# The second half of the gated block's value projection as seven block products, with spatial-weight preparation and the last statistics moved into the projection behind it

## The chip, the cores and the metric

The kernel runs on one core of one Trainium2 chip. The metric is the device time of one execution in microseconds (us), as a median of several runs. All times below come from those runs or from one execution taken by the profiler.

## The reference, cut to what matters

The program is a four-layer network on 512 tokens of width 1024: latent attention, stick-breaking attention, a gated block with a spatial mixing of tokens, and windowed attention. The change lies in the gated block alone:

```python
def gmlp_mixer(h, w_in, ln_g, ln_b, ws, bs, w_out):      # h: 512 x 1024, w_in: 1024 x 6144
    z = h @ w_in
    u, v, g = jnp.split(z, 3, axis=-1)                    # each 512 x 2048
    v = layer_norm(v, ln_g, ln_b)
    v = v.reshape(b, nc, CHUNK, A_GROUPS, A_GROUP_DIM)    # 4 chunks of 128 tokens, 16 groups of 128
    wsm = jnp.where(causal[None], ws, jnp.zeros_like(ws))
    sv = jnp.einsum('gts,bcsgd->bctgd', wsm, v) + bs.T[:, :, None]
    y = u * sv.reshape(b, s, A_WIDTH) * jax.nn.silu(g)
    return y @ w_out
```

Here h is the RMS-normed residual stream. All inputs are 32-bit floats.

## The kernel before, in words

**Matmuls in three parts.** TensorE multiplies values that are each split into a high and a low part (w_hi and w_lo for weights, a0h and a0l for activations). One product of 128x128 by 512 columns is three matmuls: high by high, high by low, low by high (`three`, L572 to L576). ScalarE (ACT) makes the high part of each weight slab with a copy (L1233), VectorE (DVE) the low part with a subtraction (L1857). Both hold two slabs of 128x1024: slot r % 2 for load r.

**Projections.** A `Linear` (L372 to L399) has groups of 512 output columns, and a group has loads of two k tiles each, four loads for K = 1024. A group fills four PSUM banks; groups alternate between banks 0 to 3 and 4 to 7. For each k tile TensorE (PE) computes four tiles, so that a group is 8 x 4 x 3 = 96 matmuls and a load 24. PE waits for `lo_ready` at each load, and at the start of group G for the readers of group G - 2, which had the same banks (L604 to L606). ACT may overwrite a slot when PE has finished the load two before (L1232: `ring_used` at least r - 1).

**Order by hand.** Every engine's program is written out in order. In the helper `linear` of ACT (L1252) and DVE (L1878), step j of group g first splits load g * 4 + j + 1, so the load after the one of this step; then, at j = 0 and 1 of every group but the first, it reads two banks each of the group before; then it takes one item of the list `extra`:

```python
split_to(L.load0 + g * L.lpg + j + 1, i)
if g and j < 2:
    reads(g - 1, range(4) if L.lpg == 1 else range(2 * j, 2 * j + 2), i)
if extra:
    extra.pop(0)()
```

With `between=True` DVE reads the last group's banks 0 and 1 with a split behind each; ACT has no such option.

**The gated block.** `g_v` (L390) is the value projection: four groups, token-major, so banks hold 128 tokens by 512 columns. ACT evicts each bank with the token's norm factor (`v_read`, L1696), DVE takes bn_stats of it (`v_stats`, L2390). `g_u` (L391) follows, with four groups that DVE reads with the norm row (`normed_to`, L1969), then the spatial product (L1057 to L1067) and `g_g`.

Beside g_v lies the preparation of the spatial weights: ACT makes high parts (`ws_hi`, L1721), DVE low parts (`ws_low`, L2396), PE multiplies them by minus one's matrix for their column sums (`ws_sums`, L1040 to L1050, eight matmuls, called ahead of k tile 6 of the second group of g_v), and DVE multiplies the four banks of sums by a gain and adjusts a bias (`ws_bias`, L2399 to L2409). The four banks of sums are those that the third group of g_v uses, so PE waits at its start: `if G == lin["g_v"].group0 + 2: pe.wait_ge(S("ws_bias"), 4)` (L599). On DVE `ws_bias` is the eighth item of `extra`, so it comes at the last step of the second group. `v_moments` and `v_shift` (first two items in g_u) join the statistics, POOL takes the root (L2796), and ACT normalizes v_g in four instructions (`v_normed`, L1713, items three to six of g_u).

**A projection by seven products is already there.** `sh_v` (L383, 1024 columns of another layer) goes by `fast` (L896), a Strassen-like scheme of Winograd's form: the operands are cut into 2x2 blocks, four sums of activation blocks and four of weight blocks are made, and seven block products of 4 k tiles x 2 tiles x 3 = 24 matmuls each replace eight. Its loads are half slabs (28 loads of 128x512, six matmuls each). The activation sums are made beside the projection ahead, `sh_k`: ACT scales activations (`gained`, L1574), DVE adds (`sums`, L2264), both split (`sums_hi` L1566, `sums_lo` L2253). The weight sums are made by transfers that add: SyncE (SP) loads four slabs after the norm of sh_k (`load_sums`, L534 to L539, issued between loads 5 and 6 of sh_k), POOL issues four adding transfers onto them (`weight_sums`, L2731 to L2739), and DVE adds twice two more (`weight_sum`, L2276). ACT evicts the first products (L1582), DVE adds the others onto them (L2285); both are called `fast_tokens` (L1578, L2278).

In sh_k only DVE reads banks; in g_v ACT reads them first and DVE works on what ACT wrote.

Of the kernel before, what the change touches and what calls it, by code (L numbers as in the profile page):

```python
# [8 lines left out]
ALU = mybir.AluOpType  # L9
# [75 lines left out]
class Fast:  # L85
# [5 lines left out]
    def __init__(self, extra, sums):  # L91
        self.extra, self.sums = extra, sums
        self.home, self.landed = {}, {}

# [38 lines left out]
def build(nc, ctx, ins, out, cols):  # L133
# [53 lines left out]
    def put(name, shape, kb, dt=F32, of=None):  # L187
# [42 lines left out]
        + [put("sv_slot3", [P, 2, T], 80)]  # L230
    kT_sh = put("kT_sh", [P, KD, T], 32)
# [134 lines left out]
    def columns(a, b, step=T):  # L366
# [16 lines left out]
        Linear("sh_v", w_sh, 8, columns(D, 2 * D), True, A0, items("h_kv"), fast=Fast(sv_slots, (s_hi, s_lo))),  # L383
# [6 lines left out]
        Linear("g_v", w_g, 8, columns(GW, 2 * GW), True, A0, items("h_g")),  # L390
# [13 lines left out]
               "sh_v": ("sums_out", 4),  # L404
               "gate1": ("g_read", 0), "g_v": ("g_read", 8), "g_u": ("g_read", 24), "g_g": ("g_read", 40)}
# [4 lines left out]
    for L in LINEARS:  # L410
# [97 lines left out]
    def _(sp_):  # L508
# [36 lines left out]
        for L in LINEARS[1:]:  # L545
# [25 lines left out]
    def _(pe):  # L571
# [13 lines left out]
        def group(L, g, i=None, before={}):  # L585
# [13 lines left out]
            if G == lin["g_v"].group0 + 2:  # L599
                pe.wait_ge(S("ws_bias"), 4)  # L600
# [295 lines left out]
        def fast(L):  # L896
# [155 lines left out]
        linear("g_v", 2, second={6: ws_sums})  # L1052
        linear("g_u")
# [143 lines left out]
    def _(act):  # L1197
# [10 lines left out]
        def split(r, i=None):  # L1208
# [353 lines left out]
        def sums_hi(qs):  # L1562
            def do():
                for q in qs:
                    act.wait_ge(S("s_ok"), q + 1)
                    act.activation(s_hi[:, q, :, :], s_f[:, q, :, :], ACT.Copy).then_inc(S("s_hi"), 1)  # L1566
            return do

        def gained(sets, name):
            def do():  # L1570
                for q in sets:
                    k0, t0 = ((4, T // 2), (0, T // 2), (0, 0), (4, 0))[q]
                    for k in range(4):
                        last = act.activation(s_f[:, q, k, :], xT[:, k0 + k, t0:t0 + T // 2], ACT.Identity, scale=gain(name, k0 + k))  # L1574
# [3 lines left out]
        def fast_tokens(L, t):  # L1578


            def evict(to, bank, m, sem):
                act.activation(to, bank, ACT.Identity, scale=nrm[:, m:m + 1]).then_inc(S(sem), 1)  # L1582

            a = ps[4 * (L.group0 % 2):4 * (L.group0 % 2) + 2]
            for j in range(Fast.N):
                split_to(L.load0 + j)
                if j == 7:
                    act.wait_ge(S("ring_used"), L.load0 + 4)
                    act.wait_ge(S("nrm_ok"), 2)
                    for m in range(2):  # L1590
                        evict(t[:, m, T:D], a[m][:, :], m, "first_out")
                    for m in range(2):
                        evict(t[:, 2 + m, 0:T], a[m][:, :], 2 + m, "first_out")
                if j == 23:
                    act.wait_ge(S("ring_used"), L.load0 + 20)
                    for m in range(2):
                        evict(t[:, m, 0:T], a[m][:, :], m, "first_out")

        linear("sh_k", None, [nothing, nothing, gained((0, 1), "h_kv"), gained((2, 3), "h_kv"), hi_two("h_sb", 0), hi_two("h_sb", 1),
                               lambda: (sums_hi((0, 1))(), hi_two("h_sb", 2)()), lambda: (sums_hi((2, 3))(), hi_two("h_sb", 3)())])  # L1600
        fast_tokens(lin["sh_v"], v_sh)
# [122 lines left out]
        linear("g_v", v_read, [nothing, nothing] + [ws_hi(q) for q in range(4)] + [nothing] * 10)  # L1724
        linear("g_u", extra=[nothing, nothing] + [v_normed(m) for m in range(MB)], near=True)
# [105 lines left out]
    def _(dve):  # L1831
# [417 lines left out]
        def sums_lo(qs):  # L2249
            def do():  # L2250
                for q in qs:
                    dve.wait_ge(S("s_hi"), 4 + q + 1)
                    dve.tensor_tensor(s_lo[:, q, :, :], s_f[:, q, :, :], s_hi[:, q, :, :], ALU.subtract).then_inc(S("s_lo"), 1)  # L2253
            return do

        def sums(qs):
# [10 lines left out]
        def weight_sum(name, p):

            b, count, read = {"t2": ("b22", None, 6), "t4": ("b21", 5, 10)}[name]
            at = lin["sh_v"].fast  # L2270
            to = at.home["t", p]
            if count:
                dve.wait_ge(S("s_ok"), count + p)
            dve.wait_ge(*at.landed[b, p])
            dve.wait_ge(S("lo_ready"), lin["sh_v"].load0 + read + 2 * p)
            dve.tensor_tensor(to[:, :, :], to[:, :, :], at.home[b, p][:, :, :], ALU.add).then_inc(S("s_ok"), 1)  # L2276

        def fast_tokens(L, t):  # L2278
# [5 lines left out]
            def add(to, bank, m, other, sem, op=ALU.add):  # L2284
                dve.scalar_tensor_tensor(to, bank[:, :], nrm[:, m:m + 1], other, ALU.mult, op).then_inc(S(sem), 1)  # L2285

            one, two = slice(0, T), slice(T, D)
            done = "sums_out"
            for j in range(Fast.N):
# [5 lines left out]
                if j == 15:  # L2295
                    dve.wait_ge(S("ring_used"), L.load0 + 12)
                    dve.wait_ge(S("first_out"), 4)
                    for m in range(2):
                        add(t[:, 2 + m, one], b[m], 2 + m, t[:, 2 + m, one], done)
                if j == 16:  # L2300
                    for m in range(2):
                        add(t[:, m, two], b[m], m, t[:, m, two], done)
                if j == 18:
                    dve.wait_ge(S("ring_used"), L.load0 + 16)
                    dve.wait_ge(S(done), 2)
                    for m in range(2):
                        add(t[:, 2 + m, two], d[m], 2 + m, t[:, 2 + m, one], done)
                if j == 19:
                    dve.wait_ge(S(done), 6)
                    for m in range(2):  # L2310
                        add(t[:, 2 + m, two], c[m], 2 + m, t[:, 2 + m, two], done, ALU.subtract)
                if j == 27:
                    dve.wait_ge(S("ring_used"), L.load0 + 24)
                    for m in range(2):
                        add(t[:, m, two], c[m], m, t[:, m, two], done, ALU.subtract)
            split_to(L.load0 + Fast.N)
            dve.wait_ge(S("ring_used"), L.load0 + Fast.N)
            for m in range(2):
                add(t[:, 2 + m, one], d[m], 2 + m, t[:, 2 + m, one], done)

        linear("sh_k", normed_to(kT_sh, 1),
               [nothing, nothing, norm(1, 1e-6, "sh_k"), sums((0,)), lambda: (sums((1, 2, 3))(), lo_two("h_sb", 0)()), lo_two("h_sb", 1),
                lambda: (sums_lo((0, 1))(), lo_two("h_sb", 2)()), lambda: (sums_lo((2, 3))(), lo_two("h_sb", 3)())], between=True)
        fast_tokens(lin["sh_v"], v_sh)
# [66 lines left out]

        def ws_low(q):
# [18 lines left out]
        linear("g_v", v_stats, [nothing, nothing, norm(2, 1e-5, "g_v")] + [ws_low(q) for q in range(4)] + [ws_bias])  # L2411
# [32 lines left out]
        linear("g_u", normed_to(ug, 2), [v_moments, v_shift], near=True)  # L2444
# [171 lines left out]
    def _(pool):  # L2616
# [178 lines left out]
        root(nrm, MB, "nrm_in", 3, "nrm_ok")  # L2795
        root(bn_rs, MB, "bn_in", 1, "bn_ok")  # L2796
# [126 lines left out]
```

## Time and profile before

| | us |
|---|---|
| median of 3 runs | 1309.9 (1309.74 to 1310.02) |
| the profiled execution, its own time | 1309.88 |
| span of that execution, first to last instruction | 1308.1 |
| PE busy | 1290.3 (99% of the span) |
| DVE busy | 787.4 (60%) |
| ACT busy | 660.3 (50%) |
| POOL busy | 349.2 (27%) |

The time is 1.8 us longer than the span. In the timeline rows each line has a start in us from the span's start, a duration in us, the engine, the source line, the operation, what it writes and reads, and how many instructions were merged; a bracket gives the idle time ahead of it and what ended it. Matmuls are pipelined, so one's duration reaches into the next: the distance between starts tells their pace. The rows themselves stand behind the diff.

### The profile page before, as it was taken

What the parts mean: (1) busy time and instruction counts of PE and PEld (TensorE: products, weight loads), DVE (VectorE), ACT (ScalarE), POOL (GpSimd) and SP (SyncE); (2) the same over time, 40 slices, a digit from 0 to 9 for tenths busy, and PEclk for the clock granted to TensorE, in tenths of its full rate; (3) what the DMA queues carried; (4) which work ended last, traced back from release to release, by engine and by line L of the source; (5) the groups of instructions that cost most, each with busy time, mean ns of one, the idle gap of its engine ahead of it and who ended that gap; (6) DMA issues with size and microseconds to landing.
All of it is one profiled execution on the core that took longest, in us unless ns stands there. A gap on an engine that the chain in (4) does not pass through costs nothing.

```text
span 1308.1 us, 17925 instructions
## 1 busy us (share of the span) xinstructions
PE 1290.3 (99%) x6454; PEld 1081.5 (83%) x6454; DVE 787.4 (60%) x1253; ACT 660.3 (50%) x1202; POOL 349.2 (27%) x397
## 2 busy tenths in 40 slices
PE   7999999999999999999999999999999999999998
PEld 6997778788888888887888888889888888888886
DVE  5646888735698235897444653335457236578843
ACT  5379888624664326997244523414244234355632
POOL 2238877400010008773000000000000000668620
PEclk9999999999999999999999999999999999999999
DMA  5332100132192232001323323331332321421111
GB/s 195 85 106 65 45 25 14 49 104 96 58 257 80 98 97 81 1 0 33 113 97 97 97 86 99 97 96 59 99 98 95 123 97 49 130 65 49 33 65 65
DMA packets 72500, 107.81 MB, mean 82 GB/s; under 512 B 3572, under 2 KB 31464, under 8 KB 72296
## 3 DMA queue, kind: packets, MB, share of 16 engines
q1 hardware_dynamic: 70128, 100.49, 24.4%
q0 software_dynamic: 2176, 6.27, 1.9%
q8 instruction: 47, 0.77, 0.3%
q14 instruction: 29, 0.24, 0.1%
q10 hardware_dynamic: 120, 0.05, 0.0%
HBM read 104.70 MB, written 2.10 MB: 82 GB/s over the span
## 4 chain that ended last, share of the span: by engine, by line
PE 91%; DVE 4%; issue 2%; ACT 1%; DMA 1%; SPq 0%; DVEq 0%; POOL 0%; ACTq 0%; POOLq 0%
PE ps L574 24%; PE ps L576 24%; PE ps L575 24%; PE ps L777 3%; PE ps L1121 2%; PE ps L973 2%; PE ps L790 1%; PE ps L963 1%; PE ps L1065 1%; PE ps L756 1%; PE ps L964 1%; PE ps L804 1%; DVE sp L2334 1%; PE ps L805 1%; DMA x_tok<-in_x 1%
## 5 line engine op out<-in xcount | busy, mean ns | idle before, releaser
L1857 DVE TENSOR_TENSOR w_lo<-stage,w_hi 128x1024 fp32r<-128x1024 f32 (+4 forms) x180 | 214.3, 1191 | 374.7 <-ACT w_hi L1233 374.5
L1233 ACT ACTIVATE w_hi<-stage 128x1024 fp32r<-128x1024 f32 (+4 forms) x180 | 182.7, 1015 | 417.8 <-PE ps L576 412.5
L574 PE MATMUL ps<-a0h,w_hi 128*128 128x512 f32 x512 | 204.6, 400 | 0.8 <-DVE q_lo L2521 0.8
L576 PE MATMUL ps<-a0h,w_lo 128*128 128x512 f32 x512 | 199.9, 390 | 0.0
L575 PE MATMUL ps<-a0l,w_hi 128*128 128x512 f32 x512 | 199.5, 390 | 0.0
L2623 POOL TENSOR_TENSOR small<-small 128x16 f32<-128x16 f32 (+2 forms) x14 | 32.3, 2313 | 387.9 <-DVE small L1941 284.4
L576 PEld LDWEIGHTS ps<-a0h,w_lo 128*128 128x128 f32 x512 | 96.1, 188 | 20.6
L574 PEld LDWEIGHTS ps<-a0h,w_hi 128*128 128x128 f32 x512 | 96.2, 188 | 20.1 <-issue 1.3
L575 PEld LDWEIGHTS ps<-a0l,w_hi 128*128 128x128 f32 x512 | 96.3, 188 | 18.3 <-issue 0.2
L574 PE MATMUL ps<-w_hi,a0h 128*128 128x512 f32 (+1 forms) x280 | 106.3, 380 | 0.1
L576 PE MATMUL ps<-w_hi,a0l 128*128 128x512 f32 (+1 forms) x280 | 104.3, 373 | 0.0
L575 PE MATMUL ps<-w_lo,a0h 128*128 128x512 f32 (+1 forms) x280 | 104.2, 372 | 0.0
L574 PE MATMUL ps<-a1h,w_hi 128*128 128x512 f32 x256 | 100.0, 391 | 0.3 <-DVE w_lo L1857 0.3
L576 PE MATMUL ps<-a1h,w_lo 128*128 128x512 f32 x256 | 99.6, 389 | 0.0
L575 PE MATMUL ps<-a1l,w_hi 128*128 128x512 f32 x256 | 99.6, 389 | 0.0
L574 PEld LDWEIGHTS ps<-w_hi,a0h 128*128 128x128 f32 x280 | 52.6, 188 | 10.1 <-issue 0.9
L575 PEld LDWEIGHTS ps<-w_lo,a0h 128*128 128x128 f32 x280 | 52.6, 188 | 9.1 <-issue 0.7
L576 PEld LDWEIGHTS ps<-w_hi,a0l 128*128 128x128 f32 x280 | 52.5, 188 | 8.5
L574 PEld LDWEIGHTS ps<-a1h,w_hi 128*128 128x128 f32 x256 | 48.0, 188 | 11.0 <-DVE w_lo L1857 0.8
L576 PEld LDWEIGHTS ps<-a1h,w_lo 128*128 128x128 f32 x256 | 48.0, 188 | 10.1
L575 PEld LDWEIGHTS ps<-a1l,w_hi 128*128 128x128 f32 x256 | 48.1, 188 | 9.8
L574 PE MATMUL ps<-yh,w_hi 128*128 128x512 f32 x128 | 49.9, 390 | 0.0
(347 smaller groups left out, 2969.5 us busy)
## 6 DMA issues: line engine op xcount, KB each, us to landing
stage<-in_a_w_in SPq DMA_DIRECT2D x48, 512.0 KB, 3.7
stage<-in_ple_w_gate SPq DMA_DIRECT2D x16, 512.0 KB, 3.3
stage<-in_sb_w_in SPq DMA_DIRECT2D x16, 512.0 KB, 3.7
stage<-in_a_w_out SPq DMA_DIRECT2D x16, 512.0 KB, 3.3
stage<-in_b_w_in SPq DMA_DIRECT2D x16, 512.0 KB, 3.7
stage<-in_w_kv_shared SPq DMA_DIRECT2D x14, 512.0 KB, 4.3
stage<-in_mla_w_in SPq DMA_DIRECT2D x8, 512.0 KB, 3.9
stage<-in_sb_w_out SPq DMA_DIRECT2D x8, 512.0 KB, 3.3
```

The source lines that it names most:

```text
L574: pe.matmul(bank, wh, mh, start=start and not seeded, stop=False, skip_group_check=seeded)
L575: pe.matmul(bank, wh, ml, start=False, stop=False, skip_group_check=seeded)
L576: return pe.matmul(bank, wl, mh, start=False, stop=stop, skip_group_check=seeded)
L756: t = pe.transpose(ps[bank][0:QK, m * P:(m + 1) * P], ring[s][:, m, :], ident)
L777: pe.matmul(ps[b][:, c:c + n], qT[s][0:QK, j * P:(j + 1) * P], kT[s][0:QK, 0:n], start=j != 0, stop=False, skip_group_check=True)
L790: t = pe.transpose(ps[3 + b][:, c + (q - j) * P:c + (q - j + 1) * P], pr[:, QRY_COL[q] + j * P:QRY_COL[q] + (j + 1) * P], ident)
L804: pe.matmul(ps[6][:, j * P:T], v_hl[h % 2][:, j, :], prT_h[:, at], start=j == 0, stop=False, skip_group_check=True)
L973: t = pe.matmul(ps[6 + s][:, j * P:T], v_pair2[:, j, :], a_T[s][:, KEY_COL[j]:KEY_COL[j] + T - j * P], start=j == 0, stop=j == MB - 1, ski ...
L1121: t = pe.matmul(ps[W_OUT][:, j * P:j * P + n], v_dup[:, e, j, :], pwT[s][:, j, 0:n], start=j == 0, stop=j == MB - 1, skip_group_check=True)
L1233: act.activation(slab(w_hi[r % 2], L, nk, w), slab(stage[q], L, nk, w), ACT.Copy).then_inc(S("hi_ready"), 1)
L1857: dve.tensor_tensor(slab(w_lo[r % 2], L, nk, w), slab(stage[stage_of[r][0]], L, nk, w), slab(w_hi[r % 2], L, nk, w), ALU.subtract)\
L2623: return pool.tensor_tensor(ap, ap, minus_half[:, 0:n], ALU.pow).then_inc(S(ready), 1)
```

## The change

g_v keeps its first two groups. Its other two become a projection of their own, `g_w`, which goes by `fast` (seven products) with outputs in v_g. The helpers of sh_v are given the projection, its semaphore offsets, its buffers and its output slices as parameters, and g_w gets the same activation sums and weight sums beside g_v. ws_hi, ws_low, ws_sums and ws_bias move from g_v into g_u, and the bn_stats of g_w's halves come in g_u as `fast_stats`. The diff, cut to its core:

```diff
+    g_f = put("g_f", [P, 4, 4, T // 2], 48)
+    g_lo = put("g_lo", [P, 4, 4, T // 2], 48, F32R)
...
-        Linear("g_v", w_g, 8, columns(GW, 2 * GW), True, A0, items("h_g")),
+        Linear("g_v", w_g, 8, columns(GW, GW + D), True, A0, items("h_g")),
+        Linear("g_w", w_g, 8, columns(GW + D, 2 * GW), True, A0, items("h_g"),
+               fast=Fast(1, 3, sv_slots, g_f, (s_hi, g_lo), lambda m, half: v_g[:, 8 + 4 * half:12 + 4 * half, m, :],
+                         lambda bank: bank[:, :].rearrange("p (g d) -> p g d", g=4))),
...
-               "sh_v": ("sums_out", 4),
-               "gate1": ("g_read", 0), "g_v": ("g_read", 8), "g_u": ("g_read", 24), "g_g": ("g_read", 40)}
+               "sh_v": ("sums_out", 4), "g_w": ("sums_out", 16),
+               "gate1": ("g_read", 0), "g_v": ("g_read", 8), "g_u": ("g_read", 16), "g_g": ("g_read", 32)}
...
@@ SyncE
-            sp_.wait_ge(S("rstd_done"), 2)
+            sp_.wait_ge(S("rstd_done"), L.fast.norm)
...
-                    if r == lin["sh_k"].load0 + 5:
-                        load_sums(lin["sh_v"])
+                    for ahead, L2 in (("sh_k", "sh_v"), ("g_v", "g_w")):
+                        if r == lin[ahead].load0 + 5:
+                            load_sums(lin[L2])
...
@@ TensorE
-            if G == lin["g_v"].group0 + 2:
+            if G == lin["g_u"].group0 + 1:
                 pe.wait_ge(S("ws_bias"), 4)
...
         def ws_sums():
 
-            G = lin["g_v"].group0
+            G = lin["g_u"].group0 + 1
             pe.wait_ge(S("ws_ok"), 4)
-            pe.wait_ge(S(group_read[G][0]), group_read[G][1])
+            pe.wait_ge(S(group_read[G - 2][0]), group_read[G - 2][1])
...
-        linear("g_v", 2, second={6: ws_sums})
-        linear("g_u")
+        linear("g_v", 2)
+        fast(lin["g_w"])
+        linear("g_u", before={6: ws_sums})
...
@@ ScalarE
-        linear("g_v", v_read, [nothing, nothing] + [ws_hi(q) for q in range(4)] + [nothing] * 10)
-        linear("g_u", extra=[nothing, nothing] + [v_normed(m) for m in range(MB)], near=True)
+        gw = lin["g_w"]
+        linear("g_v", v_read, [nothing, nothing, gained(gw, (0, 1), "h_g"), gained(gw, (2, 3), "h_g"), nothing, nothing,
+                               sums_hi(gw, (0, 1)), sums_hi(gw, (2, 3))])
+        fast_tokens(gw)
+        linear("g_u", extra=[lambda: [ws_hi(q)() for q in range(4)], nothing, nothing, nothing] + [v_normed(m) for m in range(MB)], near=True)
...
@@ VectorE
+        def fast_stats():
+
+            dve.wait_ge(S("sums_out"), gw.fast.count("sums_out", 12))
+            dve.wait_ge(S("first_out"), gw.fast.count("first_out", 6))
+            for n in range(MB):
+                for g in (2, 3):
+                    dve.bn_stats(bn_st[:, n, g, :], v_g[:, 4 * g:4 * g + 4, n, :]).then_inc(S("bn_done"), 1)
+
...
         def ws_bias():
 
-            G = lin["g_v"].group0
+            G = lin["g_u"].group0 + 1
...
-        linear("g_v", v_stats, [nothing, nothing, norm(2, 1e-5, "g_v")] + [ws_low(q) for q in range(4)] + [ws_bias])
+        gw = lin["g_w"]
+        linear("g_v", v_stats, [nothing, nothing, norm(2, 1e-5, "g_v"), sums(gw, (0,)), sums(gw, (1, 2, 3)), nothing,
+                                sums_lo(gw, (0, 1)), sums_lo(gw, (2, 3))], between=True)
+        fast_tokens(gw)
...
-        linear("g_u", normed_to(ug, 2), [v_moments, v_shift], near=True)
+        linear("g_u", normed_to(ug, 2), [fast_stats, lambda: [ws_low(q)() for q in range(4)], v_moments, v_shift, ws_bias], near=True)
...
@@ GpSimd
         root(nrm, MB, "nrm_in", 3, "nrm_ok")
+        weight_sums(lin["g_w"])
         root(bn_rs, MB, "bn_in", 1, "bn_ok")
```

## Rows read from the trace of the kernel before

**Rows 1.** the page: busy time, and engines of the chain that ended last
```profile
PE 1290.3 (99%) x6454; PEld 1081.5 (83%) x6454; DVE 787.4 (60%) x1253; ACT 660.3 (50%) x1202; POOL 349.2 (27%) x397
...
PE 91%; DVE 4%; issue 2%; ACT 1%; DMA 1%; SPq 0%; DVEq 0%; POOL 0%; ACTq 0%; POOLq 0%
```

**Rows 2.** busy time by windows: span, engines, PEclk, DMA share, GB/s
```profile
790.00:812.00 22.00, 22.00 (x98) 18.20 (x97) 7.30 (x8) 6.56 (x8) 0.00 (x0) 1.00 0.35 100
```

**Rows 3.** timeline of PE: first matmul of g_v's third group, of g_u's first two
```profile
769.18 0.39 PE L574 MATMUL ps<-w_hi,a0h 128*128 128x512 f32 x1
...
812.70 0.39 PE L574 MATMUL ps<-a0h,w_hi 128*128 128x512 f32 x1
...
834.46 0.39 PE L574 MATMUL ps<-a0h,w_hi 128*128 128x512 f32 x1
```

**Rows 4.** timeline of PE: sh_v's first matmul, the first behind sh_v (sb_gate's)
```profile
384.23 0.39 PE L574 MATMUL ps<-w_hi,a0h 128*128 128x512 f32 x1
...
422.55 0.47 PE L574 MATMUL ps<-a1h,w_hi 128*128 128x512 f32 x1
```

**Rows 5.** timeline of SP, POOL, ACT in sh_k: weight sums, the load behind
```profile
359.90 1.91 SPq L539 DMA_DIRECT2D sv_slot<-in_w_kv_shared  x4
...
368.93 5.01 POOL L2739 DMA_DIRECT2D sv_slot<-in_w_kv_shared  x4 [11.39 <-DMA sv_slot<-in_w_kv_shared]
...
370.01 1.07 ACT L1233 ACTIVATE w_hi<-stage 128x1024 fp32r<-128x1024 f32 x1 [5.00 <-DMA stage<-in_w_kv_shared]
...
388.20 2.36 ACT L1227 ACTIVATE w_hi<-sv_slot 128x512 fp32r<-128x512 f32 x4 [2.56 <-DMA sv_slot<-in_w_kv_shared]
```

**Rows 6.** timeline of ACT and DVE in sh_v: half slabs, high and low
```profile
384.49 1.16 ACT L1227 ACTIVATE w_hi<-stage 128x512 fp32r<-128x512 f32 x2 [1.15 <-PE ps L576]
...
385.48 0.68 DVE L1855 TENSOR_TENSOR w_lo<-stage,w_hi 128x512 fp32r<-128x512 f32 x1
```

**Rows 7.** timeline of ACT at g_v's end, DVE in the group behind
```profile
812.96 1.06 ACT L1233 ACTIVATE w_hi<-stage 128x1024 fp32r<-128x1024 f32 x1 [4.38 <-PE ps L576]
...
813.92 2.40 ACT L1696 ACTIVATE v_g<-ps,small 128x512 f32<-128x512 f32 x4
...
815.19 2.46 DVE L2390 BATCH_NORM_STATS2 small<-v_g 128x6 f32<-128x512 f32 x4
```

**Rows 8.** timeline of DVE behind sh_v's end
```profile
423.96 1.22 DVE L1857 TENSOR_TENSOR w_lo<-stage,w_hi 128x1024 fp32r<-128x1024 f32 x1
```

**Rows 9.** timeline of DVE at g_v's second group's end: ws_bias
```profile
764.34 2.48 DVE L2406 TENSOR_TENSOR ws_b<-ps,gains 128x512 f32<-128x512 f32 x4
```

**Rows 10.** timeline of ACT and DVE at the start of g_u's second group
```profile
834.72 1.06 ACT L1233 ACTIVATE w_hi<-stage 128x1024 fp32r<-128x1024 f32 x1 [2.38 <-PE ps L576]
...
835.81 1.23 DVE L1857 TENSOR_TENSOR w_lo<-stage,w_hi 128x1024 fp32r<-128x1024 f32 x1 [4.21 <-ACT w_hi L1233]
...
836.95 1.28 DVE L1969 TENSOR_TENSOR ug<-ps,rstd 128x512 f32<-128x512 f32 x2
```

**Rows 11.** timeline of PE: a wait for DVE, and the matmul behind it
```profile
508.31 0.50 PE L574 MATMUL ps<-a1h,w_hi 128*128 128x512 f32 x1 [0.33 <-DVE w_lo L1857]
...
508.65 0.40 PE L575 MATMUL ps<-a1l,w_hi 128*128 128x512 f32 x1
```

**Rows 12.** PE's last matmul; then windows (columns as in rows 2) behind it
```profile
1301.75 0.39 PE L576 MATMUL ps<-w_hi,o_bl 128*128 128x512 f32 x1
...
1305.50:1306.00 0.50, 0.00 (x0) 0.00 (x0) 0.00 (x0) 0.00 (x0) 0.00 (x0) 0.66 1.05 389
...
1306.00:1307.00 1.00, 0.00 (x0) 0.00 (x0) 0.00 (x0) 0.00 (x0) 0.00 (x0) 0.50 1.00 385
```

**Rows 13.** timeline of PE: the first products of the span
```profile
8.32 0.80 PE L574 MATMUL ps<-pTh,w_hi 128*128 128x512 f32 x1 [1.16 <-DVE w_lo L1851]
...
8.91 0.63 PE L575 MATMUL ps<-pTl,w_hi 128*128 128x512 f32 x1
...
12.18 0.40 PE L574 MATMUL ps<-pTh,w_hi 128*128 128x512 f32 x1
```

More of the change, by code:

```diff
@@ L89, with __init__, count @@
     N = 4 * len(SPLITS)
-    def __init__(self, extra, sums):
-        self.extra, self.sums = extra, sums
+    def __init__(self, nth, norm, extra, total, sums, out, shape):
+        self.nth, self.norm, self.extra, self.total, self.sums, self.out, self.shape = nth, norm, extra, total, sums, out, shape
         self.home, self.landed = {}, {}
+    def count(self, name, n):
+        return n + self.nth * {"sums_in": 64, "adds_in": 64, "s_hi": 8, "s_ok": 8, "s_lo": 4, "first_out": 6, "sums_out": 12}[name]
     def source(self, j):
@@ L382, in build @@
         Linear("sh_k", w_sh, 8, columns(0, D), False, A0, items("h_kv")),
-        Linear("sh_v", w_sh, 8, columns(D, 2 * D), True, A0, items("h_kv"), fast=Fast(sv_slots, (s_hi, s_lo))),
+        Linear("sh_v", w_sh, 8, columns(D, 2 * D), True, A0, items("h_kv"),
+               fast=Fast(0, 2, sv_slots, s_f, (s_hi, s_lo), lambda m, half: v_sh[:, m, half * T:half * T + T], lambda bank: bank[:, :])),
         Linear("sb_gate", w_sb, 8, columns(D, 2 * D), False, A1, items("h_sb")),
@@ L437, in build @@
                     if name in ("t", "b12"):
-                        to, landed, need = L.fast.extra[p + 2 * (name == "t")], (S("adds_in"), 64), None
+                        to, landed, need = L.fast.extra[p + 2 * (name == "t")], (S("adds_in"), L.fast.count("adds_in", 64)), None
                     else:
@@ L1560, in hi_two, with sums_hi, gained @@
             return do
-        def sums_hi(qs):
+        def sums_hi(L, qs):
             def do():
                 for q in qs:
-                    act.wait_ge(S("s_ok"), q + 1)
-                    act.activation(s_hi[:, q, :, :], s_f[:, q, :, :], ACT.Copy).then_inc(S("s_hi"), 1)
+                    act.wait_ge(S("s_ok"), L.fast.count("s_ok", q + 1))
+                    act.activation(L.fast.sums[0][:, q, :, :], L.fast.total[:, q, :, :], ACT.Copy).then_inc(S("s_hi"), 1)
             return do
-        def gained(sets, name):
+        def gained(L, sets, name):
             def do():
@@ L1573, in do, with fast_tokens, evict @@
                     for k in range(4):
-                        last = act.activation(s_f[:, q, k, :], xT[:, k0 + k, t0:t0 + T // 2], ACT.Identity, scale=gain(name, k0 + k))
+                        last = act.activation(L.fast.total[:, q, k, :], xT[:, k0 + k, t0:t0 + T // 2], ACT.Identity, scale=gain(name, k0 + k))
                     last.then_inc(S("s_hi"), 1)
             return do
-        def fast_tokens(L, t):
-            def evict(to, bank, m, sem):
-                act.activation(to, bank, ACT.Identity, scale=nrm[:, m:m + 1]).then_inc(S(sem), 1)
+        def fast_tokens(L):
+            out = L.fast.out
+            def evict(to, bank, m):
+                act.activation(to, L.fast.shape(bank), ACT.Identity, scale=nrm[:, m:m + 1]).then_inc(S("first_out"), 1)
             a = ps[4 * (L.group0 % 2):4 * (L.group0 % 2) + 2]
@@ L1588, in fast_tokens @@
                     act.wait_ge(S("ring_used"), L.load0 + 4)
-                    act.wait_ge(S("nrm_ok"), 2)
+                    act.wait_ge(S("nrm_ok"), L.fast.norm)
                     for m in range(2):
-                        evict(t[:, m, T:D], a[m][:, :], m, "first_out")
+                        evict(out(m, 1), a[m], m)
                     for m in range(2):
-                        evict(t[:, 2 + m, 0:T], a[m][:, :], 2 + m, "first_out")
+                        evict(out(2 + m, 0), a[m], 2 + m)
                 if j == 23:
@@ L1596, in fast_tokens @@
                     for m in range(2):
[L1597 to L1601, printed above, removed]
+                        evict(out(m, 0), a[m], m)
+        sv = lin["sh_v"]
+        linear("sh_k", None, [nothing, nothing, gained(sv, (0, 1), "h_kv"), gained(sv, (2, 3), "h_kv"), hi_two("h_sb", 0), hi_two("h_sb", 1),
+                               lambda: (sums_hi(sv, (0, 1))(), hi_two("h_sb", 2)()), lambda: (sums_hi(sv, (2, 3))(), hi_two("h_sb", 3)())])
+        fast_tokens(sv)
         linear("sb_gate", silu_gate)
@@ L2248, in _, with sums_lo @@
         rest_of_layer(0, 1, "h_kv")
[L2249 removed]
+        def sums_lo(L, qs):
             def do():
                 for q in qs:
[L2252 to L2256 removed]
+                    dve.wait_ge(S("s_hi"), L.fast.count("s_hi", 4 + q + 1))
+                    dve.tensor_tensor(L.fast.sums[1][:, q, :, :], L.fast.total[:, q, :, :], L.fast.sums[0][:, q, :, :], ALU.subtract)\
+                       .then_inc(S("s_lo"), 1)
+            return do
@@ L2265, in sums @@
             return do
[L2267 to L2276, printed above, removed]
@@ L2278, in fast_tokens, with weight_sum, add @@
-        def fast_tokens(L, t):
+        def fast_tokens(L):
             here, there = ps[4 * (L.group0 % 2):4 * (L.group0 % 2) + 4], ps[4 * (1 - L.group0 % 2):4 * (1 - L.group0 % 2) + 4]
             b, c, d = here[2:4], there[0:2], there[2:4]
[L2284 to L2288, printed above, removed]
+            out, count = L.fast.out, L.fast.count
+            def weight_sum(name, p):
+                other, after, read = {"t2": ("b22", None, 6), "t4": ("b21", 5, 10)}[name]
+                to = L.fast.home["t", p]
+                if after:
+                    dve.wait_ge(S("s_ok"), count("s_ok", after + p))
+                dve.wait_ge(*L.fast.landed[other, p])
+                dve.wait_ge(S("lo_ready"), L.load0 + read + 2 * p)
+                dve.tensor_tensor(to[:, :, :], to[:, :, :], L.fast.home[other, p][:, :, :], ALU.add).then_inc(S("s_ok"), 1)
+            def add(to, bank, m, other, op=ALU.add):
+                dve.scalar_tensor_tensor(to, L.fast.shape(bank), nrm[:, m:m + 1], other, ALU.mult, op).then_inc(S("sums_out"), 1)
@@ L2314, in fast_tokens @@
                     for m in range(2):
-                        add(t[:, m, two], c[m], m, t[:, m, two], done, ALU.subtract)
+                        add(out(m, 1), c[m], m, out(m, 1), ALU.subtract)
             split_to(L.load0 + Fast.N)
@@ L2318, in fast_tokens @@
             for m in range(2):
-                add(t[:, 2 + m, one], d[m], 2 + m, t[:, 2 + m, one], done)
+                add(out(2 + m, 0), d[m], 2 + m, out(2 + m, 0))
+        sv = lin["sh_v"]
         linear("sh_k", normed_to(kT_sh, 1),
-               [nothing, nothing, norm(1, 1e-6, "sh_k"), sums((0,)), lambda: (sums((1, 2, 3))(), lo_two("h_sb", 0)()), lo_two("h_sb", 1),
-                lambda: (sums_lo((0, 1))(), lo_two("h_sb", 2)()), lambda: (sums_lo((2, 3))(), lo_two("h_sb", 3)())], between=True)
-        fast_tokens(lin["sh_v"], v_sh)
+               [nothing, nothing, norm(1, 1e-6, "sh_k"), sums(sv, (0,)), lambda: (sums(sv, (1, 2, 3))(), lo_two("h_sb", 0)()), lo_two("h_sb", 1),
+                lambda: (sums_lo(sv, (0, 1))(), lo_two("h_sb", 2)()), lambda: (sums_lo(sv, (2, 3))(), lo_two("h_sb", 3)())], between=True)
+        fast_tokens(sv)
         linear("sb_gate", normed_to(sg, 1))
```

38 lines of the change are left out of this document (20 added, 18 removed).

## The prediction

> **What bounds the kernel now.** I read the page first: TensorE (PE) is busy for 99% of the span and holds 91% of the chain that ended last [rows 1]. So time goes down only where PE issues less, and any new wait of PE adds to it. Next I asked for windows inside g_v: PE is busy for the whole stretch at a granted clock of 1.00, DVE and ACT for a third of it [rows 2]. Then the timeline of PE for the pace. A matmul is listed with 0.39 us, but matmuls overlap, and that is not what one costs. From the first matmul of g_v's third group to the first of g_u are 192 matmuls in 812.70 - 769.18 = 43.52 us, 0.2267 us each, with no gap [rows 3]. A group of 96 takes 21.76 us, a full load of 24 takes 5.44, a half slab of six 1.36.
>
> **What the change takes away.** Two groups are 192 matmuls; seven products of 24 are 168. That is 24 x 0.2267 = **5.44 us less**. (By the listed 0.39 it would be 9.4, which is wrong for the reason above.) Can seven products run at PE's pace? In sh_v they do: 422.55 - 384.23 = 38.32 us for 168 matmuls, against 38.08 at the pace above [rows 4]. What surrounds g_w differs from that at two places, its start and the group after it.
>
> **What is moved or added without price.** Activation sums (gained, sums, sums_hi, sums_lo) lie beside g_v at the same steps as beside sh_k, which fed sh_v in time and had the splits for another layer to do as well. SP waits at L539 for the norm ahead of four transfers, with g_v's last two loads and all half slabs queued behind. In sh_k those transfers started at 359.90 and the load behind them came at 370.01 [rows 5]; split in 1.07 and 1.2 us it was ready at about 372.3, and PE wanted it at 384.23 - 10.88 = 373.35. That cover is 1 us; beyond it every us late is one lost. POOL issues the four adding transfers in 5.01 us [rows 5] and has nothing behind them until the statistics' root in g_u. They had landed when ACT went on at 388.20, 3.97 us into sh_v [rows 5]. fast_stats stands on DVE ahead of g_u's third slab: behind sh_v DVE was done with the second slab 2.63 us after PE went on (423.96 + 1.22 - 422.55) [rows 4, 8]; eight bn_stats of 0.62 (2.46 for four [rows 7]) bring that to 7.55, the third slab to 8.8, and PE wants it at 10.88. ws_low (four like a half slab's 0.68 [rows 6]) ends by 11.5, ws_hi on ACT before that; ws_sums is ahead of k tile 6, at 16.3, its eight matmuls are as many as before. v_normed is two steps later, with two groups of g_u still to run.
>
> **A wait at the start of g_w.** ACT now evicts g_v's last group (in sh_k it had nothing to read) before it makes the high part of g_w's third half slab, whose slot is free only when PE is through with g_v. ACT comes 0.26 us after PE's first matmul of what follows (812.96 against 812.70); four evictions are 2.40 [rows 3, 7]; the high part 0.58, the low part 0.68 [rows 6]; 0.05 to PE: 3.97. PE is through two half slabs at 2.72, so it waits 1.25. Then DVE owes, by its order, a bn_stats, a low part, two bn_stats and the low part for the fifth half slab: 3.92 + 0.62 + 0.68 + 1.23 + 0.68 + 0.05 = 7.2, where PE comes at 3.97 + 2.72 + 0.1 = 6.8, the 0.1 being what a restart costs (0.34 instead of 0.23 to the next start [rows 11]). With the overlaps I take **1.6 us** for both; ends 0.2 (as sh_v) and 2.5 (no overlap, and 0.5 from a later landing).
>
> **A wait in front of g_u's second group.** ws_sums fills the four banks of g_u's second group, so PE now waits there for ws_bias. On DVE ws_bias is the fifth item of g_u's list. Four items go with the four steps of the first group; the fifth comes at step 0 of the second, behind the split of that group's second load and behind two reads of the first group's banks. Both need the first group finished: the split's slot is free only then, and the reads ask for it. So PE stops at the end of the first group, and the whole of this chain lies bare, where before ws_bias ended about 2 us ahead of PE (764.34 + 2.48 against 769.18 [rows 3, 9]). Its price stands in the trace at the very place: PE would go on at 834.46 [rows 3]; ACT's high part starts at 834.72, DVE's low part at 835.81, the two reads at 836.95 and take 1.28 [rows 10]; four multiplications take 2.48 [rows 9]. That ends at 840.71, 6.25 late; with 0.05 to PE and 0.1 for the restart **6.4 us**. Ends 6.0 and 6.8. The fifth operation of ws_bias is not waited for.
>
> **The clock.** PE is then idle for 6.2 us. Before, it has no such pause within the work, so the price is bounded from its two ends. Behind its last matmul (ended 1302.14) the granted clock fell from 1.00 to 0.50 inside 1305.5 to 1306.0, about 3.5 us later [rows 12]; a pause of 6.2 us reaches past that. How the pace comes back shows at the span's start: eight starts from 8.91 to 12.18 took 3.27 us where 1.81 is usual, and the first 0.59 instead of 0.34 [rows 11, 13], so at about half the pace, in all 1.7 us lost. Ends: 0 (no fall) and twice that, 3.4; I take **1.7**, the one recovery that rows show. The Trainium skill (TensorE: Matmul & The Clock Gate, Part 1: The HAM clock gate (the "warmup" mystery)) states as a rule that an idle TensorE drops to half its clock and that only sustained activity releases it. By that rule the sum is the one with this term, without it the one of the first rival; the fall in rows 12 agrees, and no run here shows it for a pause between matmuls.
>
> **The sum.** -5.44 + 1.6 + 6.4 + 1.7 = +4.3 us. The profiled execution took 1309.88 (1.8 more than its span), so **1314.1**; the median of the runs, 1309.9, is the same to 0.02. The chain is PE's to the end, so nothing behind g_u gives back or adds.
>
> **Rivals.** (1) Both waits, but the clock stays up or costs nothing: +2.6, 1312.4. For it: the pause is not far longer than what the clock outlived in rows 12. Against: it is longer by almost 3 us. (2) On the other side: ws_bias comes before PE does. It has four operations, and their input is complete 5.4 us before the first group ends; if DVE reached them at step 3, as it did before in g_v, they would end in time, and only the first wait would be left: -5.44 + 1.6, **1306.0**. The point that decides is whether the fifth item runs ahead of the end of the first group; by the helper's order it can't, so this needs that I misread the list. (3) The adding transfers land late. w_g has rows three times as long as w_sh, and g_w has 1.9 us of slack (its fifth half slab is wanted at 7.2 - 1.3 = 5.9, they landed at 3.97); if they took 4 us more, PE would lose 2: 1316.2. Against: each row piece is as long as in sh_v. (4) The seven products do not shorten g_w, with all else as forecast: this would be 5 us worse, and rows 4 speak against it; I give it next to nothing.
>
> **How the numbers follow.** Forecast 0.70, rival 1 0.13, rival 2 0.09, rival 3 with all later stalls 0.08. The forecast's own range is 1312.9 to 1316.0 (first wait 1.2 to 2.0, second 6.0 to 6.8, clock 1.0 to 3.0). The range of 8 in 10 takes in rival 1 and a little of rival 3: 1312.0 to 1316.6; rival 2 stays out. What a measurement of this kernel tells from no change is about 0.2%, 2.6 us. Faster is rival 2 and little else: 0.09. Within 0.2% (up to 1312.5) are half of rival 1 and the low corner of the forecast: 0.12. Slower: 0.79.
>
> **What would show it.** In the changed kernel's timeline PE should pause about 1.2 us at g_w's third half slab with DVE's low part (L1855) as releaser, and about 6 us between g_u's first two groups with DVE's ws_bias as releaser, followed by about eight matmuls at starts 0.41 apart under a granted clock of 0.50. From g_w's first matmul to g_u's first there should be about 39.7 us. The forecast is wrong if the second pause is under 3 us, if the pace behind it is 0.23 at once, or if ACT waits for a transfer into sv_slot long after PE has run dry.

## The result and the profile after

The changed kernel takes 1315.01 us (median of six runs, 1314.44 to 1315.85), the kernel before 1309.97. The ratio is 1.0038 (95% interval 1.0027 to 1.005): slower, by 5.0 us. The profiled execution took 1314.71 us, its span is 1312.9, 4.8 more than before.

The page of the changed kernel, its busy times and the engines of the chain that ended last (before: [rows 1]):

```profile
PE 1287.7 (98%) x6430; PEld 1078.0 (82%) x6430; DVE 817.0 (62%) x1297; ACT 677.3 (52%) x1240; POOL 354.3 (27%) x401
...
PE 91%; DVE 5%; issue 2%; ACT 1%; DMA 1%; SPq 0%; DVEq 0%; POOL 0%; ACTq 0%; POOLq 0%
```

PE has 24 instructions fewer and is busy for 2.6 us less, yet the span is longer: the loss is in waits and in a slow stretch behind one of them. PE's waits, longest first (total, times, longest):

```profile
PE ps L585 <- DVE ws_b L2433: 6.1, 1, 6.1
...
PE ps L585 <- DVE w_lo L1873: 1.0, 1, 1.0
```

Before, neither stood in this view. The timeline of PE shows where they lie (a start in us, a duration in us; a bracket gives the idle time and its releaser). It runs from g_w's first matmul over its third and fifth half slab to g_u's first matmul, the last one of g_u's first group, the restart behind it, and the first of the spatial product:

```profile
767.48 0.39 PE L585 MATMUL ps<-w_hi,a0h 128*128 128x512 f32 x1
...
769.98 0.39 PE L587 MATMUL ps<-w_hi,a0l 128*128 128x512 f32 x1
771.41 0.50 PE L585 MATMUL ps<-w_hi,a0h 128*128 128x512 f32 x1 [1.04 <-DVE w_lo L1873]
...
774.03 0.39 PE L587 MATMUL ps<-w_hi,a0l 128*128 128x512 f32 x1
774.48 0.47 PE L585 MATMUL ps<-w_hi,s_hi 128*128 128x512 f32 x1
...
807.34 0.47 PE L585 MATMUL ps<-a0h,w_hi 128*128 128x512 f32 x1
...
830.89 0.39 PE L587 MATMUL ps<-a0h,w_lo 128*128 128x512 f32 x1
...
837.33 0.80 PE L585 MATMUL ps<-a0h,w_hi 128*128 128x512 f32 x1 [6.05 <-DVE ws_b L2433]
837.92 0.63 PE L586 MATMUL ps<-a0l,w_hi 128*128 128x512 f32 x1
...
840.91 0.58 PE L587 MATMUL ps<-a0h,w_lo 128*128 128x512 f32 x1
841.33 0.39 PE L585 MATMUL ps<-a0h,w_hi 128*128 128x512 f32 x1
...
904.60 1.61 PE L1078 MATMUL ps<-wsT,v_ring 128*128 x13
```

And of the kernel before, the first matmul of g_v's second group (to its third, at 769.18 [rows 3], are 96 matmuls and the eight of ws_sums) and the first of the spatial product:

```profile
745.52 0.39 PE L574 MATMUL ps<-w_hi,a0h 128*128 128x512 f32 x1
...
899.74 1.50 PE L1065 MATMUL ps<-wsT,v_ring 128*128 x12
```

Between g_w's first matmul and g_u's are 39.86 us, where 168 matmuls at 0.2267 are 38.08: 1.78 lost. From g_u's first matmul to its second group's are 29.99 us, where 96 matmuls and the eight of ws_sums (1.9, 769.18 less 745.52 and 21.76 before) are 23.66: 6.33 lost. From there to the spatial product are 67.27 us, before 899.74 - 834.46 = 65.28: 1.99 lost. With -5.44 for the products and 0.20 by which this execution was late already at g_v's start (721.80 against 721.60), that is -5.44 + 1.78 + 6.33 + 1.99 + 0.20 = 4.86 us, the whole of the difference at the spatial product (904.60 - 899.74).

The timelines of ACT and DVE around the first wait, at g_w's start:

```profile
767.68 2.42 ACT L1711 ACTIVATE v_g<-ps,small 128x512 f32<-128x512 f32 x4 [2.33 <-PE ps L587]
769.98 1.16 ACT L1240 ACTIVATE w_hi<-stage 128x512 fp32r<-128x512 f32 x2
771.09 1.15 ACT L1240 ACTIVATE w_hi<-sv_slot 128x512 fp32r<-128x512 f32 x2
```

```profile
770.66 0.69 DVE L1873 TENSOR_TENSOR w_lo<-stage,w_hi 128x512 fp32r<-128x512 f32 x1 [1.49 <-ACT w_hi L1240]
...
772.46 1.28 DVE L2409 BATCH_NORM_STATS2 small<-v_g 128x6 f32<-128x512 f32 x2
773.66 1.28 DVE L1873 TENSOR_TENSOR w_lo<-sv_slot,w_hi 128x512 fp32r<-128x512 f32 x2
```

Four evictions, then the high part, then the low part at 770.66, which PE got at 771.41. The added slabs had landed by 771.09, since ACT did not wait for them.

DVE ahead of the second wait, at the start of g_u's second group:

```profile
826.28 0.15 DVE L2457 SCALAR_TENSOR_TENSOR small<-small 128x4 f32<-128x4 f32 x1
832.46 1.23 DVE L1875 TENSOR_TENSOR w_lo<-stage,w_hi 128x1024 fp32r<-128x1024 f32 x1 [6.03 <-ACT w_hi L1246]
833.61 1.28 DVE L1987 TENSOR_TENSOR ug<-ps,rstd 128x512 f32<-128x512 f32 x2
834.81 2.47 DVE L2433 TENSOR_TENSOR ws_b<-ps,gains 128x512 f32<-128x512 f32 x4
```

DVE was idle for 6.03 us while PE worked off the first group; then the low part, the two reads and ws_bias ran one after another in front of an idle PE, with the durations of [rows 9, 10]. And the windows of that stretch (columns as in rows 2, PEclk is third from the right):

```profile
831.00:834.00 3.00, 0.28 (x2) 0.00 (x0) 1.54 (x2) 2.62 (x2) 0.00 (x0) 1.00 0.00 0
834.00:835.00 1.00, 0.00 (x0) 0.00 (x0) 1.00 (x3) 0.42 (x1) 0.00 (x0) 0.75 0.44 31
835.00:836.00 1.00, 0.00 (x0) 0.00 (x0) 1.00 (x2) 0.00 (x0) 0.00 (x0) 0.50 0.66 217
...
840.00:841.00 1.00, 1.00 (x4) 0.75 (x3) 0.00 (x0) 0.00 (x0) 0.00 (x0) 0.50 0.00 0
841.00:842.00 1.00, 1.00 (x5) 0.81 (x4) 0.00 (x0) 0.00 (x0) 0.00 (x0) 0.84 0.06 16
```

PE's last matmul ended at 831.28, the granted clock fell in the window 834 to 835, and PE restarted at half of it (1.2 GHz), with starts 0.43 apart until 841.33.

### The profile page after: what moved, and what is told of

The parts are those of the page before. It is cut to its first block, busy times and chain, and to the rows that moved or that the text cites. A ratio compares the mean times of both kernels' runs of the same rounds, so it can differ in the third digit from the quotient of the medians.

```text
span 1312.9 us, 17989 instructions
## 1 busy us (share of the span) xinstructions
PE 1287.7 (98%) x6430; PEld 1078.0 (82%) x6430; DVE 817.0 (62%) x1297; ACT 677.3 (52%) x1240; POOL 354.3 (27%) x401
## 4 chain that ended last, share of the span: by engine, by line
PE 91%; DVE 5%; issue 2%; ACT 1%; DMA 1%; SPq 0%; DVEq 0%; POOL 0%; ACTq 0%; POOLq 0%
PE ps L585 24%; PE ps L587 24%; PE ps L586 24%; PE ps L788 3%; PE ps L1134 2%; PE ps L985 2%; PE ps L801 1%; PE ps L975 1%; PE ps L976 1%; PE ps L1078 1%; PE ps L767 1%; PE ps L815 1%; DVE sp L2353 1%; PE ps L816 1%; DVE sp_l L2358 1%
## 5 line engine op out<-in xcount | busy, mean ns | idle before, releaser
L1875 DVE TENSOR_TENSOR w_lo<-stage,w_hi 128x1024 fp32r<-128x1024 f32 (+4 forms) x172 | 204.5, 1189 | 339.8 <-ACT w_hi L1246 339.5
L1246 ACT ACTIVATE w_hi<-stage 128x1024 fp32r<-128x1024 f32 (+4 forms) x172 | 174.0, 1011 | 387.2 <-PE ps L587 376.1
L585 PE MATMUL ps<-w_hi,a0h 128*128 128x512 f32 (+1 forms) x240 | 90.9, 379 | 1.2 <-DVE w_lo L1873 1.0
L587 PE MATMUL ps<-w_hi,a0l 128*128 128x512 f32 (+1 forms) x240 | 88.8, 370 | 0.0
L586 PE MATMUL ps<-w_lo,a0h 128*128 128x512 f32 (+1 forms) x240 | 88.7, 370 | 0.0
L585 PEld LDWEIGHTS ps<-w_hi,a0h 128*128 128x128 f32 x240 | 45.1, 188 | 10.0 <-DVE w_lo L1873 1.5
L586 PEld LDWEIGHTS ps<-w_lo,a0h 128*128 128x128 f32 x240 | 45.1, 188 | 7.4 <-issue 0.7
L587 PEld LDWEIGHTS ps<-w_hi,a0l 128*128 128x128 f32 x240 | 45.1, 188 | 7.0
```

Of the source, the lines that this page charges most:

```text
L585: pe.matmul(bank, wh, mh, start=start and not seeded, stop=False, skip_group_check=seeded)
L586: pe.matmul(bank, wh, ml, start=False, stop=False, skip_group_check=seeded)
L587: return pe.matmul(bank, wl, mh, start=False, stop=stop, skip_group_check=seeded)
L1246: act.activation(slab(w_hi[r % 2], L, nk, w), slab(stage[q], L, nk, w), ACT.Copy).then_inc(S("hi_ready"), 1)
L1875: dve.tensor_tensor(slab(w_lo[r % 2], L, nk, w), slab(stage[stage_of[r][0]], L, nk, w), slab(w_hi[r % 2], L, nk, w), ALU.subtract)\
```

## The experiments

Each is timed beside the kernel before on the same chip (1309.8 to 1310.0 us there). The theory: the two waits come from the order of the work, the second with a fall of the clock behind it. The rivals: DVE has too much to do in g_u's first group, wherever ws_bias stands; and a pause costs PE something at its restart that has nothing to do with the clock.

**ws_bias one step earlier (e1_bias_earlier).**

```diff
-[fast_stats, lambda: [ws_low(q)() for q in range(4)], v_moments, v_shift, ws_bias]
+[fast_stats, lambda: [ws_low(q)() for q in range(4)], v_moments, lambda: (v_shift(), ws_bias())]
```

> The changed kernel with ws_bias one step earlier on DVE (with v_shift, at the last step of g_u's first group). Order theory: PE's wait ahead of g_u's second group is there only because ws_bias stood behind work that needs the first group finished. Then it goes, and the slow clock behind it too: 1310.0 - 5.4 + 1.8 = about 1306.3 us. Load theory (DVE has too much to do in g_u's first group, bn_stats and ws_low, and is late wherever ws_bias stands): PE still waits 3 us or more, 1309 us or above.

1306.39 us, ratio 0.9972 (0.9961 to 0.9984). DVE's timeline there:

```profile
825.18 1.23 DVE L1875 TENSOR_TENSOR w_lo<-stage,w_hi 128x1024 fp32r<-128x1024 f32 x1 [3.47 <-ACT w_hi L1246]
826.32 0.15 DVE L2457 SCALAR_TENSOR_TENSOR small<-small 128x4 f32<-128x4 f32 x1
826.40 2.48 DVE L2433 TENSOR_TENSOR ws_b<-ps,gains 128x512 f32<-128x512 f32 x4
```

ws_bias is done at 828.88. PE has no gap at the seam, where its starts are 0.23 apart:

```profile
831.16 0.39 PE L585 MATMUL ps<-a0h,w_hi 128*128 128x512 f32 x1
831.39 0.39 PE L586 MATMUL ps<-a0l,w_hi 128*128 128x512 f32 x1
```

DVE's load is the same as in the change and it waits 3.47 us for ACT ahead of this; so the load theory is out, and the place in the list is what cost 8.6 us (1315.01 - 1306.39), the second wait and the slow clock together.

**The move alone (e7_move_alone).** The kernel before, with only the spatial-weight work put into g_u:

```diff
-        linear("g_v", v_stats, [nothing, nothing, norm(2, 1e-5, "g_v")] + [ws_low(q) for q in range(4)] + [ws_bias])
+        linear("g_v", v_stats, [nothing, nothing, norm(2, 1e-5, "g_v")])
...
-        linear("g_u", normed_to(ug, 2), [v_moments, v_shift], near=True)
+        linear("g_u", normed_to(ug, 2), [nothing, lambda: [ws_low(q)() for q in range(4)], v_moments, v_shift, ws_bias], near=True)
```

with ws_hi, ws_sums and PE's wait for ws_bias placed as in the change.

> The kernel before, all four groups of g_v as they were, with only ws_hi, ws_low, ws_sums and ws_bias moved into g_u as in the change (ws_bias fifth item, nothing in the place of fast_stats). Order theory: the same pause of 6.3 us and 2.0 at the slow clock, 1310.0 + 8.3 = 1318.3 us. Load theory: without the 4.8 us of fast_stats DVE is earlier by as much and the pause about 1.5 us, the clock stays, 1311.5 us.

1318.27 us, ratio 1.0062 (1.0047 to 1.0078). PE's wait is the same to the hundredth though DVE has 4.8 us less to do:

```profile
840.29 0.80 PE L574 MATMUL ps<-a0h,w_hi 128*128 128x512 f32 x1 [6.05 <-DVE ws_b L2406]
```

**The high parts first (e2_high_first).** On ACT and on DVE the third and fourth half slab of g_w are split ahead of the reads of g_v's last group:

```diff
-                               sums_hi(gw, (0, 1)), sums_hi(gw, (2, 3))])
+                               sums_hi(gw, (0, 1)), sums_hi(gw, (2, 3))], first=lambda: split_to(gw.load0 + 3))
...
-                                sums_lo(gw, (0, 1)), sums_lo(gw, (2, 3))], between=True)
+                                sums_lo(gw, (0, 1)), sums_lo(gw, (2, 3))], first=lambda: split_to(gw.load0 + 3))
```

> The changed kernel with the splits of g_w's third and fourth half slab ahead of the reads of g_v's last group, on ACT and DVE; ws_bias as changed. If the wait at g_w's start comes from ACT's evictions standing first, it goes: 1315.0 - 1.3 = 1313.7 us, and 39.9 us from g_w's first matmul to g_u's become 38.5. If the evictions and statistics are work that has to come before the fifth half slab anyway, the wait only moves there: 1314.6 to 1315 us.

1312.97 us, ratio 1.0024 (1.0014 to 1.0033), 2.0 less than the change. The timeline of ACT, and g_w's and g_u's first matmul on PE:

```profile
767.63 1.15 ACT L1240 ACTIVATE w_hi<-stage 128x512 fp32r<-128x512 f32 x2 [2.39 <-PE ps L587]
768.69 2.40 ACT L1711 ACTIVATE v_g<-ps,small 128x512 f32<-128x512 f32 x4
```

```profile
767.37 0.39 PE L585 MATMUL ps<-w_hi,a0h 128*128 128x512 f32 x1
...
805.60 0.47 PE L585 MATMUL ps<-a0h,w_hi 128*128 128x512 f32 x1
```

38.23 us from one to the other, 1.63 less than in the change and 0.15 over the bare pace: both small waits of g_w went, so the wait did not merely move to the fifth half slab. What is left of the 2.0, some 0.4 us, is not settled. The slow stretch behind the long pause, which this kernel still has, differs by more than that from execution to execution: the profiled one here (1313.9, the slowest of ten) needed 6.11 us for fourteen starts that usually take 3.17, so it lost 2.9 us where the change's lost 2.0:

```profile
835.58 0.80 PE L585 MATMUL ps<-a0h,w_hi 128*128 128x512 f32 x1 [6.05 <-DVE ws_b L2433]
...
841.69 0.40 PE L587 MATMUL ps<-a0h,w_lo 128*128 128x512 f32 x1
```

But the same edit also takes 1.9 us off e1_bias_earlier, which has no slow stretch (1306.39 to 1304.46, next), so that is not the whole of it.

**Both (e3_both).**

> Both edits, of e1_bias_earlier and e2_high_first. If the two waits are apart and add, 1306.3 - 1.3 = 1305.0 us, which is the 5.4 us of the seven products less a few tenths. If they share something, more than 1305.7.

1304.46 us (five runs, 1304.3 to 1304.83), ratio 0.9959 (0.9945 to 0.9973). This is 0.5 less than expected, and the two edits add: alone they take 8.6 and 2.0 us off the change, together 10.6. It is the fastest version, 5.5 us ahead of the kernel before, where 24 matmuls at PE's pace are 5.44. Its page, to be read beside the change's: PE is busy for 99% of a span of 1302.5 us again.

```profile
PE 1285.3 (99%) x6430; PEld 1077.5 (83%) x6430; DVE 816.4 (63%) x1297; ACT 677.3 (52%) x1240; POOL 353.8 (27%) x401
```

**Pauses of chosen length (e4_pause_short, e5_pause_mid, e6_pause_long, e8_pause_two).** To see the clock apart from the wait, DVE does added work ahead of ws_bias, in e1_bias_earlier (six, eight and eleven operations) or in the change (eight):

```diff
+            for d in range(8):
+                link(dve.tensor_tensor(tmp[d % 2][:, :], rstd[:, :], rstd[:, :], ALU.add))
             dve.wait_ge(S("bs_in"), 16)
```

> e1_bias_earlier with eight added DVE additions of 128x512 into tmp ahead of ws_bias (some 5.3 us, of which DVE has 2.4 to spare), so that PE pauses about 2.9 us ahead of g_u's second group. Clock theory: the granted clock stays at 1.00, as the pause is shorter than the 3.2 to 3.5 us behind which it was seen to fall, and starts are 0.23 apart at once: 1306.3 + 2.9 = 1309.2 us. Restart theory (each longer pause costs 2 us anew, whatever the clock): 1311.2 us.

> The same with eleven additions, so a pause of about 4.9 us. Clock theory: the clock falls within the pause and PE restarts at half pace, losing about 2 us: 1306.3 + 4.9 + 2.0 = 1313.2 us. If what follows the pause in the changed kernel is due to DVE's last operation of ws_bias and not to the clock: the same loss here and in e4_pause_short.

> The changed kernel with eight added DVE additions ahead of ws_bias: the pause grows by their 5.3 us to about 11.6. Clock theory: one fall and one recovery, the loss behind the pause stays about 2 us: 1315.0 + 5.3 = 1320.3 us. If the loss grows with the pause in proportion (2.0 of 6.3), 1322 us.

> e1_bias_earlier with six added DVE additions instead of eight. By the runs with eight (pause 3.4 us) and eleven (5.6 us) each is 0.72 us, so PE pauses 2.0 us. Clock theory: no fall in any execution, no spread as with eight: 1306.4 + 2.0 + 0.1 for the restart = 1308.5 us, all runs within 0.5 us. Restart theory (2 us anew behind any longer pause): 1310.5 us.

PE's wait for ws_b in the profiled execution of each, in that order (eight, eleven, eight on the change, six):

```profile
PE ps L585 <- DVE ws_b L2435: 3.4, 1, 3.4
```

```profile
PE ps L585 <- DVE ws_b L2435: 5.6, 1, 5.6
```

```profile
PE ps L585 <- DVE ws_b L2435: 11.9, 1, 11.9
```

```profile
PE ps L585 <- DVE ws_b L2435: 2.0, 1, 2.0
```

| pause, us | median, us | ratio (95%) | runs, us, and mean granted clock of each |
|---|---|---|---|
| none (e1_bias_earlier) | 1306.39 | 0.9972 (0.9961 to 0.9984) | 1306.03 to 1306.66 |
| 2.0 | 1308.96 | 0.9995 (0.9986 to 1.0005) | six at 1308.45 to 1309.05 (0.999, 1.0), four at 1310.14 to 1310.63 (0.997, 0.998) |
| 3.4 | 1311.51 | 1.0015 (1.0006 to 1.0025) | 1309.92 and 1310.1 (1.0), four at 1311.4 to 1311.53 (0.997, 0.998), four at 1312.61 to 1313.24 (0.996) |
| 5.6 | 1314.35 | 1.0032 (1.0019 to 1.0045) | 1313.97 to 1314.76 (0.996 to 0.998) |
| 11.9 | 1320.0 | 1.0078 (1.006 to 1.0096) | 1319.65 to 1321.29 (0.994 to 0.996) |

The restart theory is out: in six of ten executions with 2.0 us and two of ten with 3.4 us the time is that of the kernel without a pause plus the pause (1306.39 + 2.0 = 1308.4, + 3.4 = 1309.8) and 0.1 to 0.7 more, at a mean clock of 0.999 or 1.0. The profiled execution with 3.4 us is one of these, and PE's second start there comes 0.34 us behind the first, 0.1 more than usual:

```profile
834.36 0.50 PE L585 MATMUL ps<-a0h,w_hi 128*128 128x512 f32 x1 [3.42 <-DVE ws_b L2435]
834.70 0.40 PE L586 MATMUL ps<-a0l,w_hi 128*128 128x512 f32 x1
```

DVE's last operation of ws_bias runs behind the pause in that execution too (834.34 to 836.63), so it is not what slows PE. The clock theory is right in kind: the other executions have a lower mean clock and take 1.4 to 3.2 us more. The windows of the execution with 5.6 us show it as in the change:

```profile
834.00:835.00 1.00, 0.00 (x0) 0.00 (x0) 0.97 (x3) 0.32 (x1) 0.00 (x0) 1.00 0.03 8
835.00:837.00 2.00, 0.22 (x1) 0.23 (x2) 1.97 (x4) 0.00 (x0) 0.00 (x0) 0.55 0.00 0
837.00:840.00 3.00, 3.00 (x8) 2.32 (x9) 3.00 (x2) 0.00 (x0) 0.00 (x0) 0.50 0.00 0
```

The loss does not grow with the pause: 1320.0 - 1306.4 - 11.9 = 1.7 us with the longest, 1314.35 - 1306.4 - 5.6 = 2.4 with the one before. But what was expected of the two short pauses was wrong: they were to leave the clock alone, and part of their executions have a lower mean clock and the loss that goes with it. The pause with eight additions was also half a microsecond longer than planned, as an addition took 0.72 us with its chain and not 0.66.

## Why the prediction was right, point by point

The forecast was 1314.1 us and slower, with two waits and a fall of the clock; measured are 1315.0 and all three, each in its place and with the releaser that was named: pauses of 1.04 and 6.05 us, then eight starts 0.43 us apart (0.41 forecast), and 39.86 us for g_w (39.7 forecast).

- **The gain.** 24 matmuls by the distance of starts, 5.44: the version without the waits gained 5.5. The 9.4 of the listed durations would have been wrong by 4.
- **The wait at g_w's start.** 1.6 forecast, 1.78 measured. The chain of four evictions, high part and low part gave 1.25 against 1.20 (771.41 - 769.98 = 1.43, less the usual 0.23); then 0.22 at the fifth half slab, where the sum had 0.4. The other 0.36 comes in small pieces, of which the sum had one restart of 0.1: 0.10 and 0.08 behind the two waits, 0.11 ahead of g_u's first matmul, and hundredths.
- **The wait ahead of g_u's second group.** 6.4 forecast, 6.33 measured. Its terms were taken from the same operations at the same place of the kernel before, and the move alone shows it by itself, 8.3 us with the clock, as expected.
- **The clock.** 1.7 forecast, 1.99 in this execution. The rival in which the clock stays up fell: it came down 3.2 us into a pause of 6.05. That 1.7 came so near is in part luck: it is one recovery, read at the span's start, and behind the same pause of 6.05 us the profiled executions of e2_high_first and e7_move_alone lost 2.9 and 2.8. Of the 0.6 us between the forecast and the profiled execution, 0.3 is this term, 0.2 the wait at g_w's start and 0.2 was lost before g_v, less 0.1 at the second wait. The median lies 0.3 higher still; no trace shows why, but the six executions go from a mean clock of 0.997 (1314.44) to 0.995 (1315.85).
- **The range.** The lowest and highest terms named for the forecast's own range add up to 1312.6 and 1316.2, not 1312.9 and 1316.0; the measurement lies inside both.
- **What was costed at nothing.** fast_stats, ws_low, ws_hi and v_normed made no wait: no other releaser stands among PE's waits in this stretch, and DVE was idle for 6.03 us ahead of the seam. The slab behind the weight sums came later than forecast, high part at 753.92, low part ended at 756.24 (755.01 + 1.23). PE wanted it two loads into g_v's second group, at 767.48 - 21.76 + 10.88 = 756.60: 0.4 us of cover where the forecast had 1.0, so this was nearer to a third wait than the sum says. The added slabs were in time. The rows of ACT and DVE:

```profile
753.92 1.06 ACT L1246 ACTIVATE w_hi<-stage 128x1024 fp32r<-128x1024 f32 x1 [5.72 <-DMA stage<-in_a_w_in]
```

```profile
755.01 1.23 DVE L1875 TENSOR_TENSOR w_lo<-stage,w_hi 128x1024 fp32r<-128x1024 f32 x1 [1.73 <-ACT w_hi L1246]
```

- **The rival on the other side**, ws_bias ahead of PE, was a wrong reading of the list, as the prediction said, but the one-line edit makes it true: 1306.0 worked out, 1306.39 measured.

The rule of the Trainium skill (TensorE: Matmul & The Clock Gate, Part 1: The HAM clock gate (the "warmup" mystery)), that an idle TensorE drops to half its clock and needs activity to get it back, is borne out here between matmuls too: 1.00 to 0.50 inside the pause and back 4.0 us behind the restart in the change.

## What to carry to other kernels

When a step is moved in an order written by hand, look at what stands ahead of it on its engine and whether that needs the very work that waits for the step; here one place in a list was worth 8.6 us, more than the arithmetic saved. Cost a saved matmul by the distance between starts, not by its listed duration. And count a pause of an otherwise busy TensorE with the slow clock behind it: in the five traces with pauses of 5.6 to 11.9 us it cost 1.6 to 2.9 us more than its length.

## What was not expected of the hardware

A pause of TensorE shorter than any behind which the clock was seen to fall can cost the slow pace too. With PE idle for 2.0 us four of ten executions had a lower mean clock (0.997 or 0.998) and took about 1.6 us more, with 3.4 us eight of ten, with 5.6 us and more all, and without a pause none of seven. At 3.4 us the loss came in steps of about 1.5 and 2.9 us (1310.0, 1311.5, 1312.9), so the same program differs by up to 3.3 us from run to run. For these two pauses only the mean clock and the time show this: both profiled executions kept their clock, and when it fell in the slower ones, no trace shows.

Five traces have a fall of the clock. The fall is read from the granted clock in windows of 0.25 us, the return from PE's starts, the loss from these starts against 0.2267 us each:

| kernel | pause, us | fall, us behind PE's last matmul | usual pace, us behind the restart | loss, us |
|---|---|---|---|---|
| e5_pause_mid | 5.6 | 4.0 | 5.3 | 2.6 |
| the change | 6.05 | 3.2 | 4.0 | 2.0 |
| e2_high_first | 6.05 | 5.3 | 6.1 | 2.9 |
| e7_move_alone | 6.05 | 5.1 | 6.0 | 2.8 |
| e6_pause_long | 11.9 | 4.9 | 3.4 | 1.6 |

The moment of the fall and of the return differs with the same pause, and the loss goes with the return. In the longest pause the clock was up until about 836.16, 4.9 us behind PE's last matmul (ended 831.27), by this window:

```profile
835.00:837.00 2.00, 0.00 (x0) 0.00 (x0) 1.90 (x4) 0.00 (x0) 0.00 (x0) 0.79 0.67 244
```

If the fall comes as late behind 2.0 us, PE had restarted by then; this is argued and not shown.
